# A decoder trunk with expert retrieval: V rows gathered as 8 tokens by 16 picks and summed on TensorE's four column groups

## The reference

```python
def peer(h, w_q, sub_keys, u_tab, v_tab):
    ...
    def block(xb):                       # 128 tokens
        q = (xb @ w_q).reshape(tb, PEER_HEADS, 2, PEER_D_KEY // 2)
        s = jnp.einsum('thcd,hckd->thck', q, sub_keys, ...)
        top_s, top_i = lax.top_k(s, kk)
        cand = top_s[:, :, 0, :, None] + top_s[:, :, 1, None, :]
        cand_idx = top_i[:, :, 0, :, None] * PEER_N_KEYS + top_i[:, :, 1, None, :]
        best_s, best_pos = lax.top_k(cand.reshape(tb, PEER_HEADS, kk * kk), kk)
        expert = jnp.take_along_axis(cand_idx.reshape(...), best_pos, axis=-1)
        gate = jax.nn.softmax(best_s, axis=-1)
        act = jax.nn.gelu(jnp.einsum('td,thkd->thk', xb, u_tab[expert], ...), approximate=False)
        w = (gate * act).astype(xb.dtype)
        return jnp.einsum('thk,thkd->td', w, v_tab[expert])

for l in range(DEPTH):                   # 2 layers, x is 512 x 1024, float32
    h = rms_norm(x, attn_norm_w[l])
    proj = h @ w_in[l]                   # attention and linear-attention inputs
    ...
    x = x + mix @ w_out[l]
    h = rms_norm(x, ffn_norm_w[l])
    x = x + peer(h, peer_w_q[l], peer_sub_keys[l], peer_u[l], peer_v[l])
```

## Time and profile before

| | |
|---|---|
| median of 3 runs | 3281.9 us (3280.04 to 3284.26) |
| profiled execution, its own time | 3277.48 us |
| span of the profiled execution | 3275.7 us |
| TensorE matmuls (PE) | 2674.0 us busy, 82% |
| VectorE (DVE) | 2236.5 us busy, 68% |
| GpSimd (POOL) | 2178.2 us busy, 66% |
| ScalarE (ACT) | 750.7 us busy, 23% |
| gathers' DMA queue | 1073.87 MB, 85.1% of the 16 engines' span |

### The profile page before, as it was taken

How to read it: one execution, slowest core, us unless ns; L and a number is a source line. 1 busy time by engine, 2 the same in 40 slices (tenths; PEclk the granted TensorE clock), 3 DMA queues, 4 the chain that set the end, 5 groups by cost and what they waited for, 6 DMA issues and landing times.

```text
span 3275.7 us, 26155 instructions
## 1 busy us (share of the span) xinstructions
PE 2674.0 (82%) x7328; PEld 1257.3 (38%) x7328; DVE 2236.5 (68%) x4922; ACT 750.7 (23%) x1676; POOL 2178.2 (66%) x2074
## 2 busy tenths in 40 slices
PE   7876678998987858998888777899888787777778
PEld 3444333344444423343435433344435443222223
DVE  1549974569759995467858997457966997444443
ACT  2321121223221221223222112122322121111111
POOL 0024677777776677777776677777776666777775
PEclk9888889999999989999999989999999898999999
DMA  5248999999999999999999999999999999999998
GB/s 190 78 147 297 335 351 400 406 407 371 372 403 380 338 352 388 406 406 407 377 385 385 358 362 352 407 406 406 372 374 406 360 358 357 409 409 410 409 409 328
DMA packets 351442, 1185.41 MB, mean 362 GB/s; under 512 B 37666, under 2 KB 38212, under 8 KB 351044
## 3 DMA queue, kind: packets, MB, share of 16 engines
q0 software_dynamic: 294912, 1073.87, 85.1%
q1 hardware_dynamic: 56388, 109.88, 9.0%
HBM read 1181.52 MB, written 2.10 MB: 361 GB/s over the span
## 4 chain that ended last, share of the span: by engine, by line
DVE 25%; POOL 23%; DMA 18%; PE 16%; issue 16%; ACT 1%; DVEq 0%; POOLq 0%
POOL v_ring L479 11%; POOL u_ring L479 11%; DMA u_ring<-in_peer_u,experts 10%; PE peer_acc L1275 8%; DMA v_ring<-in_peer_v,experts 8%; DVE u_ring L1003 5%; PE act_bank L1062 4%; DVE work L763 2%; DVE work L752 2%; DVE xs L1013 2%; PE dve_banks L1062 1%; DVE work L760 1%; DVE work L749 1%; DVE work L942 1%; DVE work L944 1%
## 5 line engine op out<-in xcount | busy, mean ns | idle before, releaser
L1275 PE MATMUL peer_acc<-v_ring,diag 128*128 128x512 f32 x3712 | 1826.7, 631 | 540.1 <-DMA v_ring<-in_peer_v,experts 282.9
L479 POOL DMA_INDIRECT u_ring<-in_peer_u,experts x1024 | 1094.6, 1069 | 583.6 <-issue 300.6
L479 POOL DMA_INDIRECT v_ring<-in_peer_v,experts x1024 | 1078.1, 1053 | 497.9 <-issue 241.2
L1003 DVE SCALAR_TENSOR_TENSOR u_ring<-u_ring,h 128x1024 f32<-128x1024 f32 x768 | 941.3, 1226 | 558.0 <-DMA u_ring<-in_peer_u,experts 543.6
L1275 PEld LDWEIGHTS peer_acc<-v_ring,diag 128*128 128x128 f32 x3712 | 692.0, 198 | 1559.3 <-issue 860.9
L680 ACT ACTIVATE diag<-ident,wts 128x128 f32<-128x128 f32 x928 | 339.9, 396 | 1142.5 <-PE peer_acc L1275 928.0
L1003 DVE SCALAR_TENSOR_TENSOR u_ring<-u_ring,dve_banks 128x1024 f32<-128x1024 f32 x256 | 312.6, 1221 | 253.9 <-DMA u_ring<-in_peer_u,experts 251.3
L1062 PE MATMUL act_bank<-w_ring,hT 128*128 128x512 f32 x768 | 348.5, 601 | 0.7 <-ACT hT L519 0.7
L1062 PEld LDWEIGHTS act_bank<-w_ring,hT 128*128 128x128 f32 x768 | 148.9, 195 | 190.1 <-issue 188.8
L1149 PE MATMUL act_bank<-hT,w_ring 128*128 128x256 f32 x768 | 173.9, 381 | 0.0
L1149 PEld LDWEIGHTS act_bank<-hT,w_ring 128*128 128x128 f32 x768 | 147.2, 192 | 38.6 <-issue 20.7
(11 more groups left out here) (161 smaller groups left out, 1596.1 us busy)
## 6 DMA issues: line engine op xcount, KB each, us to landing
w_ring<-in_w_in SPq DMA_DIRECT2D x24, 2048.0 KB, 18.8
w_ring<-in_peer_w_q SPq DMA_DIRECT2D x16, 2048.0 KB, 18.3
w_ring<-in_w_out SPq DMA_DIRECT2D x8, 2048.0 KB, 18.9
u_ring<-in_peer_u,experts POOLq DMA_INDIRECT x1024, 9.9
v_ring<-in_peer_v,experts POOLq DMA_INDIRECT x1024, 9.8
xs<-in_x SPq DMA_DIRECT2D x4, 512.0 KB, 7.1
keysT<-in_peer_sub_keys SPq DMA_DIRECT2D x2, 1024.0 KB, 16.6
out<-xs SPq DMA_DIRECT2D x4, 512.0 KB, 6.8
```

Of the source, the lines that this page charges most:

```text
L479: pool.indirect_dma_start(ring[:, n % depth, :], None, table, bass.IndirectOffsetOnAxis(ap=experts[:, tile % TILES, e:e + 1], axis=0),).th ...
L1003: tell(nc.vector.scalar_tensor_tensor(out=row, in0=row, scalar=1.0, in1=h, op0=ALU.mult, op1=ALU.mult, accum_out=dots[:, c % 2, s:s + 1]), ...
L1275: ins = nc.tensor.matmul(peer_acc[:, j * 512:(j + 1) * 512], diag[:, (v_count(c, s) - 1) % DIAGS, :], v_ring[:, n % V_RING, j * 512:(j + 1 ...
```

## The change

A V gather no longer takes one pick of 128 tokens, but 16 picks of 8 tokens (`BLOCKS` = 16 such blocks in a chunk). Partition p then holds pick p mod 16 of the block's token p div 16. So the row numbers and the weights have to be turned from tokens-by-picks to that order: VectorE spreads them over 8 x 16 columns with all but the own token's entry zero (`spread`), TensorE multiplies with a 0/1 matrix `block_of` into a PSUM bank of its own (`slot_bank`), and VectorE copies the row numbers to `v_index` (`index`, for the next chunk, at slots 6, 8 and 10) and the weights, each put into its token's column of a 128x32 block, to `v_wts` (`begin`, at slots 0 and 1).

`slot_v` is then four matmuls with the same 128x32 weights on the four column groups of TensorE, each with a quarter (256 columns) of the gathered rows. The sum of token group a and column quarter j lies in partitions 32j and columns 256a of `peer_acc`, so `add_tile` adds it in 16 pieces of 32x256. The diagonals and VectorE's V rows go, `ACT_BANKS` goes from 3 to 2 for the new bank, and POOL waits for `index_ready` at a chunk's first V gather.

```diff
-DIAGS = 4
-ACT_BANKS = 3
+ACT_BANKS = 2
 DVE_BANKS = 3
-V_EVERY = 8
+PICK_TOKENS = 8
+COL_TILE = 32
 LEAD = 10
...
+    BLOCKS = P // PICK_TOKENS
+    PER_TILE = COL_TILE // PICK_TOKENS
+    COL_TILES = P // COL_TILE
+    V_COLS = D // COL_TILES
+    SPREAD_AT, FLIP_AT, INDEX_AT = 6, 8, 10
...
-        diag = sb("diag", [P, DIAGS, P])
+        block_of = sb("block_of", [P, BLOCKS])
+        token_of = sb("token_of", [P, PICK_TOKENS])
+        place_of = sb("place_of", [P, PER_TILE, COL_TILE])
+        spread = sb("spread", [P, PICK_TOKENS, TOPK])
+        v_index = sb("v_index", [P, 2, BLOCKS], U32)
+        v_wts = sb("v_wts", [P, 2, BLOCKS, COL_TILE])
...
+        slot_bank = ctx.enter_context(nc.psum_tensor("slot_bank", [P, 512], F32))
+        index_bank, wts_bank = slot_bank[:, 0:BLOCKS], slot_bank[:, BLOCKS:2 * BLOCKS]
...
                 next(parts)
             for s in range(SLOTS):
                 slot_u(0, s)
+                index(0, s)
             done = 0
             for n in range(CHUNKS * SLOTS):
                 c, s = divmod(n, SLOTS)
                 if c + 1 < CHUNKS:
                     slot_u(c + 1, s)
-                if s == 0:
-                    begin(c)
+                begin(c, s)
+                if c + 1 < CHUNKS:
+                    index(c + 1, s)
...
                         n = c * SLOTS + s
+                        if s == 0:
+                            pool.wait_ge(index_ready, c + 1)
                         if n >= V_RING:
-                            old_c, old_s = divmod(n - V_RING, SLOTS)
-                            pool.wait_ge(v_added if by_vector(old_c, old_s) else v_used, v_count(old_c, old_s))
-                        gather(v_rows, v_ring, V_RING, v_landed, c, s)
+                            pool.wait_ge(v_used, n - V_RING + 1)
+                        gather(v_rows, v_ring, V_RING, v_landed, n, v_index[:, c % 2, s:s + 1])
...
-            def begin(c):
-                act.wait_ge(u_used, (c + 1) * SLOTS)
-                nc.scalar.activation(acts[:, c % 2, :], dots[:, c % 2, :], ACT.Gelu).then_inc(act_ready, 1)
-
-            def slot_v(c, s):
+            def begin(c, s):
                 if s == 0:
-                    act.wait_ge(wts_ready, c + 1)
-                if by_vector(c, s):
-                    return
-                n = v_count(c, s) - 1
-                if n >= DIAGS:
-                    act.wait_ge(v_used, n - DIAGS + 1)
-                nc.scalar.activation(diag[:, n % DIAGS, :], ident[:], ACT.Copy,
-                                     scale=wts[:, c % 2, s:s + 1]).then_inc(diag_ready, 1)
-
-            interleave(front, lambda c, s: None, slot_v, begin)
+                    act.wait_ge(u_used, (c + 1) * SLOTS)
+                    nc.scalar.activation(acts[:, c % 2, :], dots[:, c % 2, :], ACT.Gelu).then_inc(act_ready, 1)
+
+            interleave(front, lambda c, s: None, lambda c, s: None, begin, lambda c, s: None)
...
             def add_tile(tile):
 
-                dve.wait_ge(v_used, v_done(tile))
-                v = xs[:, tile % TILES, :]
-                tell(nc.vector.tensor_tensor(v, v, peer_acc[:], ALU.add), peer_added, "peer_added")
-
-            def begin(c):
-                if c % PH == 0 and c > 0:
-                    add_tile(c // PH - 1)
+                dve.wait_ge(v_used, (tile + 1) * PH * SLOTS)
+                for a in range(COL_TILES):
+                    tokens = slice(a * COL_TILE, (a + 1) * COL_TILE)
+                    for j in range(COL_TILES):
+                        v = xs[tokens, tile % TILES, j * V_COLS:(j + 1) * V_COLS]
+                        ins = nc.vector.tensor_tensor(v, v, peer_acc[j * COL_TILE:(j + 1) * COL_TILE,
+                                                                     a * V_COLS:(a + 1) * V_COLS], ALU.add)
+                tell(ins, peer_added, "peer_added")
+
+            def over_tokens(ap):
+
+                return ap.unsqueeze(1).to_broadcast([P, PICK_TOKENS, TOPK])
+
+            own_token = token_of[:].unsqueeze(2).to_broadcast([P, PICK_TOKENS, TOPK])
+
+            def index(c, s):
+
                 tile, head = divmod(c, PH)
-                dve.wait_ge(act_ready, c + 1)
-                tell(nc.vector.tensor_tensor(wts[:, c % 2, :], acts[:, c % 2, :], gates[:, tile % TILES, head, :],
-                                             ALU.mult), wts_ready, "wts")
+                if s == SPREAD_AT:
+                    rows = experts[:, tile % TILES, head * TOPK:(head + 1) * TOPK]
+                    tell(nc.vector.tensor_tensor(spread[:], over_tokens(rows), own_token, ALU.mult),
+                         spread_ready, "spread")
+                if s == INDEX_AT:
+                    dve.wait_ge(slot_filled, 2 * c + 1)
+                    if c >= 2:
+                        dve.wait_ge(v_used, (c - 1) * SLOTS)
+                    tell(nc.vector.tensor_copy(v_index[:, c % 2, :], index_bank), index_ready, "index")
+
+            def begin(c, s):
+                tile, head = divmod(c, PH)
+                if s == 0:
+                    if c % PH == 0 and c > 0:
+                        add_tile(tile - 1)
+                    dve.wait_ge(act_ready, c + 1)
+                    link(nc.vector.tensor_tensor(wts[:, c % 2, :], acts[:, c % 2, :],
+                                                 gates[:, tile % TILES, head, :], ALU.mult))
+                    tell(nc.vector.tensor_tensor(spread[:], over_tokens(wts[:, c % 2, :]), own_token, ALU.mult),
+                         spread_ready, "spread")
+                if s == 1:
+                    dve.wait_ge(slot_filled, 2 * c + 2)
+                    if c >= 2:
+                        dve.wait_ge(v_used, (c - 1) * SLOTS)
+                    full = [P, COL_TILES, PER_TILE, COL_TILE]
+                    tell(nc.vector.tensor_tensor(
+                        v_wts[:, c % 2].rearrange("p (a r) t -> p a r t", r=PER_TILE),
+                        wts_bank.rearrange("p (a r) -> p a r", r=PER_TILE).unsqueeze(3).to_broadcast(full),
+                        place_of[:].unsqueeze(1).to_broadcast(full), ALU.mult), wts_ready, "wts")
 
...
-            def slot_v(c, s):
-                if not by_vector(c, s):
-                    return
-                tile, n = c // PH, c * SLOTS + s
-                dve.wait_ge(v_landed[n % V_RING], 16 * (n // V_RING + 1))
-                v = xs[:, tile % TILES, :]
-                tell(nc.vector.scalar_tensor_tensor(out=v, in0=v_ring[:, n % V_RING, :],
-                                                    scalar=wts[:, c % 2, s:s + 1], in1=v,
-                                                    op0=ALU.mult, op1=ALU.add), v_added, "v_added")
-
-            interleave(front, slot_u, slot_v, begin)
+            interleave(front, slot_u, lambda c, s: None, begin, index)
             add_tile(LAYERS * TILES - 1)
...
+            def index(c, s):
+
+                if s == FLIP_AT:
+                    pe.wait_ge(spread_ready, 2 * c + 1)
+                    if c > 0:
+                        pe.wait_ge(wts_ready, c)
+                    nc.tensor.matmul(index_bank, spread[:].rearrange("p t k -> p (t k)"), block_of[:],
+                                     start=True, stop=True).then_inc(slot_filled, 1)
+
+            def begin(c, s):
+
+                if s == 0:
+                    pe.wait_ge(spread_ready, 2 * c + 2)
+                    pe.wait_ge(index_ready, c + 1)
+                    nc.tensor.matmul(wts_bank, spread[:].rearrange("p t k -> p (t k)"), block_of[:],
+                                     start=True, stop=True).then_inc(slot_filled, 1)
+
             def slot_v(c, s):
-                if by_vector(c, s):
-                    return
+
                 tile, head = divmod(c, PH)
                 n = c * SLOTS + s
-                e = head * TOPK + s
-                last = head == PH - 1 and v_count(c, s) == v_done(tile)
-                if e == 0 and tile > 0:
-                    pe.wait_ge(peer_added, tile)
+                a, r = divmod(s, PER_TILE)
+                if s == 0:
+                    pe.wait_ge(wts_ready, c + 1)
+                    if head == 0 and tile > 0:
+                        pe.wait_ge(peer_added, tile)
                 pe.wait_ge(v_landed[n % V_RING], 16 * (n // V_RING + 1))
-                pe.wait_ge(diag_ready, v_count(c, s))
-                for j in range(D // 512):
-                    ins = nc.tensor.matmul(peer_acc[:, j * 512:(j + 1) * 512], diag[:, (v_count(c, s) - 1) % DIAGS, :],
-                                           v_ring[:, n % V_RING, j * 512:(j + 1) * 512],
-                                           start=(e == 0), stop=last)
+                for j in range(COL_TILES):
+                    ins = nc.tensor.matmul(
+                        peer_acc[j * COL_TILE:(j + 1) * COL_TILE, a * V_COLS:(a + 1) * V_COLS],
+                        v_wts[:, c % 2, s, :], v_ring[:, n % V_RING, j * V_COLS:(j + 1) * V_COLS],
```

(4 more changed lines are left out.)

41 lines of the change are left out of this document (19 added, 22 removed).

## The result

The change made the kernel slower: 3322.95 us as the median of 4 runs (3321.19 to 3329.65) against 3281.6 us before (3280.04 to 3284.26), a ratio of 1.0134 with a 95% interval of 1.0115 to 1.0152. The profiled execution took 3321.19 us with a span of 3319.5, against 3277.48 and 3275.7 before. The forecast was 3271, so it had the wrong sign, and the range up to 3312 did not hold the time.

The account below looks back on a forecast made before the run. Bounds: DMA at 409 GB/s in the last stage, VectorE or POOL in slower stretches. Terms 11 - 7 - 15 + 3 + 2 - 4 = -10 gave 3267.5 profiled, median 3271 us; own range 3255 to 3288, with rivals 3240 to 3312.

Parts of the forecast that it names:

- VectorE's own work: VectorE-bound stretches: 0.91 us less a chunk over 11.8 chunks, but longer sums and added small instructions; together +11 us.
- If a quarter of the partitions cost a quarter: Tile's sum on VectorE: pieces of 32x256 at some 0.15 us apiece, +4 in place of +17 at three tile ends.
- POOL held less: POOL-bound stretches, 14 chunks: without VectorE's V row behind a dot, gathers stretch less; -7 us, at most 26 gained.
- V buffers held in the recoveries: Three recoveries like 1218 to 1310: V rows at 0.65 us on TensorE end POOL's 4.9 us waits; -15 (0 to -28).
- rival C: TensorE's four column groups do not overlap, a V row stays at 1.7 us: about 3295 us; chance 0.08.
- term 4: First front: TensorE stands 2.5 us for ScalarE's two banks, +3 (0 to 6); beside the gathers it is hidden.
- term 5: Tile ends 8, 24, 40, 56: the 6.9 us sum and what follows overshoot 9.3 us of buffer slack; +2 us.
- The end, -4: Run's end: V rows used as gathers land, last about 3261, then a 6.9 us sum until 3268.3, not 3272.3.
- A: Chunk starts: first V row comes too late and holds V ring and POOL, worse at lower clock; +48, 3319; chance 0.15.
- D: POOL-bound stretches: the whole shortage is VectorE's V rows and TensorE's hold, and goes; 3248 (half) to 3225; chance 0.11.
- E: V gathers: 16 rows of one token gather more slowly than one pick of 128 tokens; +29, 3300; chance 0.08.

Follow-up runs that it names:

- the kernel without V rows: The kernel before with all 16 V rows of a chunk on TensorE through diagonals, none on VectorE (V_EVERY = 17): 3246.24 us, 0.9895.
- all banks with one sum: The change with three banks for both engines, turned values unused, and the tile's sum as one 128x1024 instruction: 3262.1 us, 0.9943, at a granted clock of 0.714.
- the long sum alone: The change with three banks for both engines, turned values unused, the sixteen-piece sum kept: 3296.3 us, 1.0044.
- the missing bank alone: The change with the tile's sum as a single 128x1024 instruction, ScalarE's two banks kept: 3285.3 us, 1.0016.

## Why the prediction was wrong

The forecast was -10 us and the profiled execution took 44 more. Of the 54 us between them, some 31 are terms 4 and 5 (the missing bank and the sum outside the routing, taken as hidden by the gathers), and 31 are terms 2 and 3 (gains that did not come); the rest came out some 9 better than forecast. Term by term, against the profiled execution of before.

1. **VectorE's own work: right.** Forecast -0.91 us a chunk; the nine routing chunks without a tile end gave -11.2, 1.2 each. Against the kernel without V rows the same nine are 13.5 longer, 1.5 each, for the 1.76 that I added. The sum's +17 at three ends is +15.8, with the gain of those chunks in it. "If a quarter of the partitions cost a quarter" was rightly left: 32x256 took 417 ns.
2. **POOL held less, -7: wrong.** The chunks bound by POOL took as long without the V rows as with them. A gather stretched beside a dot and a V row was a true row, but V rows do not lengthen the gathers in the mean: one takes POOL 1100 ns in these chunks without the rows and 1103 with them. The step that failed is the reading that VectorE's V rows hold POOL. In the change those chunks are even 12 us longer. The sentence of the Trainium skill that this term cites ("SBUF — State Buffer", SBUF: two separate sides) has a condition that the prediction leaves out: with two SBUF inputs a VectorE instruction locks the port only against a GpSimd instruction that reads SBUF. A gather takes its row numbers out of SBUF, but no run shows whether that makes it one; the spreads, with two SBUF inputs, did not lengthen the chunks bound by POOL.
3. **V buffers held in the recoveries, -15: wrong.** The row was mis-sized in what it bounds. TensorE's records came as estimated (eight in 0.64 us at the full clock, 1.08 at the lower), and four groups overlap, so rival C was out. But the recoveries went from 268.1 to 265.8 only. In the one at 1229 POOL still waited 3.6 us for V buffers (4.9 before); the rest of its 92 us are gathers (70) and the gaps ahead of them (19), so it had no more to gain than this wait. In the whole run its waits for V buffers did not fall either, 239.6 us for 234.0 (last line):

```profile
POOL u_ring L472 <- issue: 10.1, 33, 0.3
POOL v_ring L472 <- issue: 8.8, 29, 0.3
POOL v_ring L472 <- PE peer_acc L1313: 3.6, 3, 1.9
...
POOL v_ring L472 <- PE peer_acc L1313: 239.6, 178, 9.7
```

4. **Two banks, +3 in the first front: under-sized, +8.** The first wait was sized rightly (2.05 for 2.5), but there are two such waits, and part of the records behind each ran at the lower of the two clock levels: the 8.80 us for 7.11 above.
5. **"Beside the gathers this is hidden by the gathers" (term 4) and "It overshoots by little: +2" (term 5): here the forecast failed.** The first is wrong by itself: with the single sum in both versions, two banks cost 23 us (3262 to 3285), 8 of them in the first front and 12 at the three tile ends outside the routing. The second gave the slack of a tile's end, sized at 9.3 us, to the sum alone. But TensorE's stop stands just ahead of the sum, in the same buffers' time. In the table, against all banks with one sum, the three chunks lose 4.5 us by the long sum alone (144.6), 12.1 by the missing bank alone (152.2) and 29.2 by both (169.3), where 4.5 and 12.1 make 16.6. A sum is 5.7 us longer, and a stop is 6.5 to 7.0 us of standing and 1.4 to 2.9 of slow records. So the buffers cover some 4 to 5 us at such an end, whichever comes, and they do it once. In the kernel before the long sum cost these chunks nothing. The fourth end outside the routing, chunk 57, has no front's part beside it and lost 0.2.
6. **The end, -4:** -1.7. From VectorE's product (`wts`) to the first row were 2.1 us, where the prediction has 2.5, but the last row ended 22.0 after the product, where it has 19.5. The rows took 1.08 us, not 0.65, and still waited for their gathers in between.

```profile
3289.43 3.42 PE L1313 MATMUL peer_acc<-v_ring,v_wts 128*32 128x256 f32 x32 [0.84 <-DVE v_wts L1020]
...
3307.07 2.31 PE L1313 MATMUL peer_acc<-v_ring,v_wts 128*32 128x256 f32 x16 [0.20 <-DMA v_ring<-in_peer_v,v_index]
...
3309.51 6.88 DVE L982 TENSOR_TENSOR xs<-xs,peer_acc 32x256 f32<-32x256 f32 x16 [20.13 <-PE peer_acc L1313]
```

(The sum's 3271.9 us rounds to 3272, not to 3271; nothing hangs on it.)

Of the rivals, A came near by its price (3319), but by luck: it put the loss at every second chunk's start, and the chunks bound by VectorE without a tile end got shorter. Its sign, POOL waiting for V at a chunk's start, shows at the tile ends (the 8.49 us above), where the sum and the stop are the cause. What it had right is that the clock would fall. The rule of the Trainium skill named there ("TensorE: Matmul & The Clock Gate", Part 1) agrees with the trace, 0.944 to 0.714; the run at 0.714 that beats the kernel before by 20 us shows that the fall by itself was not the price; in the change it made the records behind a stop slow, as in term 4. D is out, since gathers stayed at 1.1 us in the stretch at 782 and the time rose. E is out too: the last stage kept 408 GB/s.

Open: why the chunks bound by POOL are 12 us longer in the change, and longer still in all its variants (407 to 415). In the step from 3246 to 3262 they are 19 of the 25 us between the profiled executions. In the change a gather takes POOL 1130 ns there in the mean (1103 before), and 280 gathers begin in these chunks instead of 274; that says where the 12 us are, but not why, and the mean of one front alone varies as much (1087 to 1115 before). It is not the spreads. Open too, whether ScalarE's two banks alone would cost as much in the kernel before: no run has that.

## What to carry over

When a change takes a buffer from a ring and lengthens a step elsewhere, look for the place where both fall into the same slack, and subtract from it once. An engine that takes its instructions in order and waits (here ScalarE, for a chunk's last dot) holds up everything behind it in its queue, however idle it is on average (here 13% busy), and that made its missing bank dear. And try the parts of a change alone: here taking the V rows from VectorE was worth 36 us with one constant, and the machinery around it cost twice that.

## What was not expected of the hardware

- A VectorE instruction of 32x256 out of PSUM took 417 ns, one of 128x256 424: the partitions saved nothing, so this sum, split by partition groups, cost by its number of pieces.
- TensorE's records of one kind took 0.64 or 1.08 us a V row, 3.70 or 6.55 us a half product, by the granted clock (1.00 or 0.50 and between); yet a mean granted clock of 0.714 went with the change and with a version that is 20 us faster than the kernel before.
- 256 more spreads of 0.29 us cost 8.6 us in all: about their own time in the chunks bound by VectorE, and nothing in the chunks bound by POOL. Nor did POOL's gathers get shorter in the mean when VectorE's V rows of 1.28 us went (1100 ns for 1103).
